# Four calls of small matmuls move from the recurrence of a decoder layer to the last two steps of the inversion ahead of it

## What is computed

```
def step(S, inp):
    r_t, w_t, k_t, v_t, kk_t, a_t = inp
    sa = jnp.einsum('bhvk,bhk->bhv', S, -kk_t)
    S = (S * w_t[:, :, None, :] + sa[..., None] * (kk_t * a_t)[:, :, None, :]
         + v_t[..., None] * k_t[:, :, None, :])
    return S, jnp.einsum('bhvk,bhk->bhv', S, r_t)
```

## Time and profile before

| what | value |
|---|---|
| time, median of 3 runs | 1521.6 us (1521.47 to 1523.23) |
| the profiled execution's own time | 1519.59 us |
| its span, first to last instruction | 1517.9 us |
| granted TensorE clock, mean | 0.986 of full speed |
| PE busy | 1464.3 us, 96% of the span |
| DVE, ACT, POOL busy | 985.0, 695.9, 378.2 us |
| HBM traffic | 130 GB/s over the span |

### The profile page before, as it was taken

One profiled execution on the slowest core, in us unless ns is written; L12 is line 12 of the kernel. 1 busy time (PEld: TensorE's weight loads), 2 busy tenths in 40 slices (PEclk: granted clock), 3 DMA queues, 4 the chain that ended last, 5 costly groups with the idle time before them and its releaser, 6 DMA issues.

```text
span 1517.9 us, 33992 instructions
## 1 busy us (share of the span) xinstructions
PE 1464.3 (96%) x13374; PEld 1409.3 (93%) x13374; DVE 985.0 (65%) x1579; ACT 695.9 (46%) x1188; POOL 378.2 (25%) x407
## 2 busy tenths in 40 slices
PE   7999999999989999999999999989999899999995
PEld 7999998899867999999999999979998689999995
DVE  4444435588476687775577776466865777877644
ACT  5333334765645543334443334366565465333332
POOL 4222363010532422220412222300115323222100
PEclk9999999999999999999999999999999999999998
DMA  8544543443214555444544545434521444555351
GB/s 221 150 144 149 168 149 88 126 128 101 55 34 134 157 160 151 146 141 150 159 137 142 151 152 156 152 88 123 129 78 33 123 121 136 165 150 167 126 166 35
DMA packets 318938, 198.82 MB, mean 131 GB/s; under 512 B 7792, under 2 KB 303760, under 8 KB 318832
## 3 DMA queue, kind: packets, MB, share of 16 engines
q1 hardware_dynamic: 315120, 190.69, 43.1%
q0 software_dynamic: 3712, 6.62, 2.1%
HBM read 188.50 MB, written 8.78 MB: 130 GB/s over the span
## 4 chain that ended last, share of the span: by engine, by line
PE 85%; DVE 7%; ACT 3%; issue 2%; DVEq 1%; DMA 0%; POOL 0%; SPq 0%; POOLq 0%; ACTq 0%
PE bank L2120 24%; PE bank L2122 23%; PE bank L2121 23%; DVE wlo L2613 2%; PE bank L2207 1%; DVE rlo L2644 1%; ACT whi L2410 1%; ACT z L1183 1%; PE bank L2212 1%; PE bank L764 1%; PE bank L752 1%; DVE raw L1578 1%; PE bank L2171 1%; PE bank L853 1%; PE bank L458 1%
## 5 line engine op out<-in xcount | busy, mean ns | idle before, releaser
L2410 ACT ACTIVATE whi<-raw 128x1024 fp32r<-128x1024 f32 x340 | 358.2, 1059 | 471.9 <-PE bank L2122 455.7
L2613 DVE TENSOR_TENSOR wlo<-raw,whi 128x1024 fp32r<-128x1024 f32 x340 | 421.2, 1243 | 230.1 <-ACT whi L2410 229.3
L2120 PE MATMUL bank<-rhi,whi 128*128 128x322 f32 x984 | 306.5, 311 | 0.0
L2122 PE MATMUL bank<-rhi,wlo 128*128 128x322 f32 x984 | 305.9, 311 | 0.0
L2121 PE MATMUL bank<-rlo,whi 128*128 128x322 f32 x984 | 304.8, 310 | 0.0
L2120 PE MATMUL bank<-xh,whi 128*128 128x320 f32 x912 | 286.2, 314 | 4.6 <-DVE xl L2787 3.5
L2121 PE MATMUL bank<-xl,whi 128*128 128x320 f32 x912 | 283.0, 310 | 0.0
L2122 PE MATMUL bank<-xh,wlo 128*128 128x320 f32 x912 | 282.9, 310 | 0.0
L2882 POOL TENSOR_TENSOR hl<-scratch,hh 128x320 f32 x88 | 146.9, 1669 | 495.4 <-DVE scratch L2734 379.7
L2120 PE MATMUL bank<-hh,whi 128*128 128x320 f32 (+1 forms) x704 | 218.4, 310 | 0.5 <-DVE wlo L2613 0.5
L2121 PE MATMUL bank<-hl,whi 128*128 128x320 f32 (+1 forms) x704 | 217.4, 309 | 0.0
(11 more groups left out here) (421 smaller groups left out, 1888.8 us busy)
## 6 DMA issues: line engine op xcount, KB each, us to landing
raw<-in_ffn_wg SPq DMA_DIRECT2D x88, 512.0 KB, 3.8
raw<-in_ffn_wu SPq DMA_DIRECT2D x88, 512.0 KB, 3.8
raw<-in_ffn_wd SPq DMA_DIRECT2D x88, 512.0 KB, 3.6
raw<-in_w_in SPq DMA_DIRECT2D x60, 512.0 KB, 3.8
raw<-in_w_out SPq DMA_DIRECT2D x16, 512.0 KB, 6.1
raw<-in_state_C SPq DMA_DIRECT2D x8, 512.0 KB, 6.1
out_s_C<-raw SPq DMA_DIRECT2D x8, 512.0 KB, 4.1
ring<-in_state_wkv POOLq DMA_DIRECT2D x8, 256.0 KB, 5.5
```

The source lines that it names most:

```text
L2120: pe.matmul(out, w_hi, hi, start=start, stop=False)
L2122: return pe.matmul(out, w_lo, hi, start=False, stop=stop)
L2410: act.activation(whi[:, slot, :], raw[:, slot, :], ACT.Copy).then_inc(hi_ready.sem, 1)
L2613: dve.tensor_tensor(wlo[:, slot, :], raw[:, slot, :], whi[:, slot, :].bitcast(F32), ALU.subtract).then_inc(lo_ready.sem, 1)
```

## The change

The four calls leave the stages and are issued in steps 25 and 26 of the inversion, two in each, behind whatever else these steps hold (`OWN_AT`). They write into `bank[7]`, which the last transposes of step 24 used, and the wait for ACT's copy of those transposes moves with the first call. ACT's copy of the bank into `s0sum` goes to the start of stage 0. What follows in the samples' chain moves one stage ahead: `samples_r` from stage 2 to stage 1, `samples_u` and the copies behind it from stage 3 to stage 2, DVE's addition L1662 from the end of stage 2 to the end of stage 1. `samples_y` stays in stage 3. No instruction is added or removed; no DMA moves.

```diff
-            sums = bank[3][:, :].rearrange("p (j s t) -> p j s t", j=NJ, s=2)
+            sums = bank[7][:, :].rearrange("p (j s t) -> p j s t", j=NJ, s=2)
...
                     last.then_inc(r_mm.sem, 1)
-                    if c == 1:
-                        samples_memory_products(pe, L, 1)
                     if c == 2:
-                        samples_memory_products(pe, L, 3)
-                    if c == 3:
                         samples_u(pe, L)
...
                 if c == 1:
-                    samples_memory_products(pe, L, 2)
-                if c == 2:
                     samples_r(pe, L)
...
                 last.then_inc(y_mm.sem, 1)
-                if c == 0:
-                    samples_memory_products(pe, L, 0)
...
+                if n in OWN_AT:
+                    for j in range(NJ // 2):
+                        samples_memory_products(pe, L, 2 * OWN_AT.index(n) + j)
             grow(pe, L, NSTEP - 1)
             recurrence(pe, L)
...
+        OWN_AT = (25, 26)
...
         def scalar_recurrence(act, L, split_hi):
             for c in range(NPC):
+                if c == 0:
+                    act.wait_ge(samples_mm.sem, samples_mm.by(L, 1))
+                    act.activation(s0sum[:, :, :, :].rearrange("p j s t -> p (j s t)"), bank[7][:, :],
+                                   ACT.Copy).then_inc(s0sum_ready.sem, 1)
                 if c == 2:
-                    act.wait_ge(samples_mm.sem, samples_mm.by(L, 1))
-                    act.activation(s0sum[:, :, :, :].rearrange("p j s t -> p (j s t)"), bank[3][:, :],
-                                   ACT.Copy).then_inc(s0sum_ready.sem, 1)
-                if c == 3:
                     act.wait_ge(samples_mm.sem, samples_mm.by(L, 3))
...
-                if c == 3:
+                if c == 2:
                     dve.wait_ge(samples_mm.sem, samples_mm.by(L, 3))
                     dve.tensor_copy(uv[PART[0], NPC, :, 0, :], heads4(bank[3])[PART[0]]).then_inc(us_ready.sem, 1)
...
-                if c == 2:
+                if c == 1:
                     dve.wait_ge(samples_mm.sem, samples_mm.by(L, 2))
                     tt(rsb_s[:, :, :], heads4(bank[3]), yr[:, slot(NPC), :, :], ALU.add).then_inc(rs_ready.sem, 1)
```

## The result

The changed kernel took 1527.35 us (median of 12 runs, 1525.51 to 1530.21), the kernel before 1522.33 (12 runs beside them, 1518.31 to 1526.37): a ratio of 1.0032 with the interval 1.0021 to 1.0042, 5.0 us slower. The forecast was 1522.7 and its range ended at 1526.8, so it was wrong. The profiled execution took 1527.9 us.

What follows compares the result with a forecast made beforehand. PE was taken as the chain ahead of U(0), PE and DVE alternating in the stages. Each layer loses 3.16 and gains 2.62 us; two layers add 1.1 to 1519.59, plus 2.0 for the median: 1522.7 us, range 1520.5 to 1526.8.

Steps and rivals of the forecast that it cites:

- The calls in steps 25 and 26: End of the inversion: the two moved pairs make U(0) start 1.26 + 1.9 = 3.16 us later per layer.
- The bounds 2.5 and 3.9: Delay of U(0) per layer: 2.5 us if both pairs overlap their neighbours more, 3.9 with no overlap.
- The stages: From U(0) to U(3): 2.62 us gained per layer, 1.76 from the stall and 0.86 from all four calls.
- The stalls: PE's "issue" waits in stages 1 and 2, 1.76 us in layer 0, expected gone; rival that they stay: chance 0.17.
- The reason given: PE used up 256-instruction blocks before the next came; after the move each block holds 5.4 to 5.9 us of work.
- The clock: Rival: the moved 16-column calls lower TensorE's clock just ahead of U(0); 1525 to 1527.3 us, chance 0.20.
- The argument against it: Against a clock fall at the moved calls: they follow each other three to four times faster than the small L458.
- the price: Clock fall in the stages: 1.15 us per layer for one 3.3 us stretch, 2.3 for two, one behind each pair.
- the prediction's own formula: Cost of a clock fall in the stages: 0.7 (PE's share of their time) x length of the stretch / 2.
- The upper end of the rival's time: Whole kernel if the clock falls behind each pair of calls: 1522.7 + 4.6 = 1527.3 us.
- the 2.0 us that the sum added: Whole kernel: the median of the runs lies 2.0 us above the profiled execution, so the same was added to 1520.7.
- the third rival: The calls hide in steps 25 and 26 after all; 1521.3 or so at a loss of 2.5 us; chance 0.11.

Runs made afterwards that it cites:

- wide_after: The changed kernel with each matmul of its four calls run over up to 64 columns instead of 16: 1519.98 us, ratio 0.998 to the kernel before.
- wide_before: The kernel before with its calls widened to up to 64 columns at their old places: 1521.28 us, ratio 0.999.
- late_wout: The kernel before with wide calls and the loads of `w_out` held back until U(2) has been computed: 1518.04 us, ratio 0.9968.
- second_wide: The changed kernel with only the second pair of calls (step 26) widened to up to 64 columns: 1526.51 us, ratio 1.0019.
- shift_wide: The kernel before with wide calls and 24 spare matmuls (96 PE instructions, results unused) in step 21: 1520.4 us, ratio 0.9986.

## Why the prediction was wrong

- **The calls in steps 25 and 26** were priced right: 3.16 us per layer forecast, 3.06 measured where the clock holds (wide_after). The bounds 2.5 and 3.9 held.
- **The stages** too: 2.62 forecast, 2.7 measured. Stage 2 with `samples_u` in front of U(2), and S(2) 1.6 us behind it, came as estimated (U(2) at 474.98, S(2) at 476.55 after the change, in layer 0, where the clock was back at 1.00).
- **The stalls** went, as forecast, and not for the lower clock: wide_after has none at 1.00. The reason given fits the trace: for the 256 instructions from U(0) to y(1), estimated at 5.9 us, PE takes some 5.8 in wide_after's profile. Instruction blocks of 256 and their lateness behind `w_out`'s loads are shown by the runs on the shifted list and on the late loads. The Trainium skill, page "Runtime: NRT & Kernel Launch", section "Instruction fetch mechanics", is right here on the 256, and its "mostly hidden" does not hold while the DMA engines are full: 2.1 us for a block in wide_before.
- **The clock** is the step that failed. It stood as a rival with a chance of 0.20 and a price of 1.15 to 2.3 us per layer. It was the case, and it cost 7.4 us (1527.35 - 1519.98), 3.7 per layer. Two things were wrong. The argument against it was that the calls follow each other three to four times faster than the L458 of the earlier trace rows. Pace was the wrong measure, as the widened calls show: the same pace and the same busy time with more columns held the clock. And the price was taken from a stretch of 3.3 us. The fall here lasted some 10 us; put into the prediction's own formula, 0.7 x 10.2 / 2 gives 3.6 per layer, so the length is what was mis-sized. U(0) and the first stages lie in the fall, where PE waits for DVE at every step, and where dense matmuls followed at once (second pair wide), it was over after 6.8; that these waits are the reason was not tried by itself. In layer 0 the fall also nearly doubled the second pair of calls, 3.53 us for 1.97. The upper end of the rival's time, 1527.3, is all but the measured one, and that is luck: it adds 4.6 to 1522.7, where the runs show 7.4 on top of 1520.0.
- **The base.** The sum was made against one profiled execution of before, in which the clock held in the stages. Profiles of the same list up to step 26 (wide_before, late_wout) show it at 0.50 from about 456.5 us, ahead of any call, so the kernel before falls in some executions. Its runs say the same: of the 35 beside wide_after the fastest took 1518.65 us at a mean granted clock of 0.991, and the seven slowest, from 1525.75 us on, have 0.977 to 0.981. A straight line through the 35 gives 0.67 us for each 0.001 of clock. Wide_after's runs have 0.0037 more on average, by this estimate 2.5 us. Measured, it is 2.4 us faster than before, although its stretch is 0.4 us per layer longer in the profiles. So the 2.0 us that the sum added for the median of the runs is, by this estimate, time lost to falls, and the forecast is 2.7 too high for a list in which the clock holds. This is a relation between runs; no run changed the clock alone.
- **One sum** in the third rival does not come out as it is written: 1522.5 - 0.9 is 1521.6. The 1521.3 beside it is right, from 1519.59 + 2.0 - 2 x 0.12, and no chance rests on the slip.

## What to carry to other kernels

Before small matmuls are moved next to each other, put a price on the clock behind them, not only on their own time, and take it from a run. Here two pairs of calls with 16 columns a matmul cost 3.7 us per layer by the clock, more than the 3.06 by which they delayed U(0), though PE was busy without a gap and the instructions followed closely. Try the same calls with more columns: here 64 cost no more time than 16 (1.97 us a pair), and the clock held. A stall of "issue" that lies in the same place of the list in every profile, while DMA is full, may be cured by moving the transfer and not the work: holding back `w_out` gave 3.2 us over wide_before, where moving the four wide calls gave 1.3.

## What was not expected of the hardware

With one and the same program the clock falls in one layer and not in the other (second_wide: 0.50 for 6.8 us in layer 0, none in layer 1), and single runs lie up to 12 us apart, in step with their mean granted clock (1518.55 us at 0.989, 1530.89 at 0.977). And 64 records of matmuls on one half of the partitions, into the same columns each time, took 3.94 us at a granted clock of 1.00, where 64 records of calls, on both halves in turn and into columns of their own, take 1.97. The halves decide, not the columns: the 48 records of spare matmuls in shift_wide, on both halves in turn and into the same columns each time, took 1.61 us at 1.00.
